# Step-size product of a gated state-space block: high and low weight columns side by side, with the next unit's two tiles computed block by block beside it

## The reference

```python
u = rms_norm(x, ln1[i]) * (1.0 + scale1) + shift1
...
proj = u @ w_in
gl, cb, cc, cx, z, xbc, dt = jnp.split(proj, split_at, axis=-1)
...
xbc = jax.nn.silu(causal_depthwise_conv(xbc, ssm_conv_w) + ssm_conv_b.astype(xbc.dtype))
...
dt = jax.nn.softplus(dt.astype(jnp.float32) + dt_bias.astype(jnp.float32))
a = -jnp.exp(a_log.astype(jnp.float32))
y = ssd_scan(xs * dt[..., None], dt * a, bs, cs)
```

## Time and profile before

| | us |
|---|---|
| median of 3 runs | 2229.18 (2227.27 to 2230.26) |
| the profiled execution, its own time | 2227.39 |
| its span in the trace | 2225.5 |
| PE busy | 2191.5 (98%) |
| VectorE busy | 1297.4 (58%) |
| ScalarE busy | 858.3 (39%) |
| mean granted clock of TensorE | 0.994 |

### The profile page before, as it was taken

One profiled execution on the slowest core, in us unless ns is written; L12 is line 12 of the kernel. 1 busy time (PEld: TensorE's weight loads), 2 busy tenths in 40 slices (PEclk: granted clock), 3 DMA queues, 4 the chain that ended last, 5 costly groups with the idle time before them and its releaser, 6 DMA issues.

```text
span 2225.5 us, 28686 instructions
## 1 busy us (share of the span) xinstructions
PE 2191.5 (98%) x10938; PEld 1829.6 (82%) x10938; DVE 1297.4 (58%) x1831; ACT 858.3 (39%) x1223; POOL 25.4 (1%) x24
## 2 busy tenths in 40 slices
PE   7999999999999999999999999999999999999998
PEld 5888888888888898888888888889878678888887
DVE  5677777777673475434475344354777756434344
ACT  5655555543222342322343222234455444222224
POOL 0000000000000000000000000000001000000000
PEclk9999999999999999999999999999999899999999
DMA  7423223224543334223223322223121012232321
GB/s 262 126 82 105 97 96 105 101 76 158 183 151 101 104 116 133 95 95 96 92 95 98 111 94 96 95 95 93 40 77 39 20 33 82 95 98 98 107 85 67
DMA packets 208141, 222.10 MB, mean 100 GB/s; under 512 B 9413, under 2 KB 200330, under 8 KB 205994
## 3 DMA queue, kind: packets, MB, share of 16 engines
q1 hardware_dynamic: 206362, 210.26, 29.1%
q10 hardware_dynamic: 1680, 10.49, 1.2%
HBM read 218.57 MB, written 2.16 MB: 99 GB/s over the span
## 4 chain that ended last, share of the span: by engine, by line
PE 93%; DVE 3%; DMA 2%; ACT 1%; issue 1%; ACTq 0%; DVEq 0%; SPq 0%
PE G L560 25%; PE G L561 25%; PE G L562 25%; PE G L611 2%; PE G L612 2%; PE G L613 2%; PE G L1050 1%; PE X L763 1%; PE X L1067 1%; DMA araw<-in_w_ada 1%; PE G L574 1%; PE G L576 1%; PE G L575 1%; PE X L1057 1%; PE X L1033 1%
## 5 line engine op out<-in xcount | busy, mean ns | idle before, releaser
L560 PE MATMUL G<-ahi,whi 128*128 128x512 f32 x1480 | 587.8, 397 | 0.1
L562 PE MATMUL G<-ahi,wlo 128*128 128x512 f32 x1480 | 577.8, 390 | 0.0
L561 PE MATMUL G<-alo,whi 128*128 128x512 f32 x1480 | 577.5, 390 | 0.0
L1874 DVE TENSOR_TENSOR wlo<-raw,whi 128x2048 fp32r<-128x2048 f32 (+3 forms) x172 | 386.9, 2249 | 237.4 <-ACT whi L1208 234.5
L1208 ACT ACTIVATE whi<-raw 128x2048 fp32r<-128x2048 f32 (+3 forms) x176 | 330.1, 1876 | 443.0 <-PE G L562 423.4
L560 PEld LDWEIGHTS G<-ahi,whi 128*128 128x128 f32 x1480 | 278.9, 188 | 58.8 <-issue 2.1
L561 PEld LDWEIGHTS G<-alo,whi 128*128 128x128 f32 x1480 | 279.0, 188 | 58.4 <-issue 1.9
L562 PEld LDWEIGHTS G<-ahi,wlo 128*128 128x128 f32 x1480 | 278.6, 188 | 58.6
L560 PE MATMUL G<-hhi,whi 128*128 128x512 f32 x784 | 305.8, 390 | 0.5 <-issue 0.5
L562 PE MATMUL G<-hhi,wlo 128*128 128x512 f32 x784 | 305.0, 389 | 0.0
L561 PE MATMUL G<-hlo,whi 128*128 128x512 f32 x784 | 305.0, 389 | 0.0
(11 more groups left out here) (422 smaller groups left out, 2844.8 us busy)
## 6 DMA issues: line engine op xcount, KB each, us to landing
raw<-in_w_in SPq DMA_DIRECT2D x43, 1024.0 KB, 5.1
raw<-in_w_up SPq DMA_DIRECT2D x38, 1024.0 KB, 5.3
raw<-in_w_down SPq DMA_DIRECT2D x32, 1024.0 KB, 5.1
raw<-in_w_gate SPq DMA_DIRECT2D x22, 1024.0 KB, 5.1
braw<-in_w_ada SPq DMA_DIRECT2D x12, 1024.0 KB, 5.3
raw<-in_w_in SPq DMA_DIRECT2D x20, 512.0 KB, 4.5
araw<-in_w_ada ACTq DMA_DIRECT2D x8, 1024.0 KB, 18.0
bc<-acum_dram SPq DMA_DIRECT2D x8, 1024.0 KB, 6.9
```

Source lines behind the costliest of these rows:

```text
L560: pe.matmul(bank[:], wh[:, j, f], rh[:, j, :], start=(j == 0), stop=False)
L561: pe.matmul(bank[:], wh[:, j, f], rl[:, j, :], start=False, stop=False)
L562: last = pe.matmul(bank[:], wl[:, j, f], rh[:, j, :], start=False, stop=(j == k - 1))
L1874: tt(wlo[s][:, 0:n], raw[s][:, 0:n], r32(whi[s][:, 0:n]), ALU.subtract).then_inc(lo_split, 1)
```

## The change

The step-size product takes two matmuls for each block instead of three. The high and the low part of its 32 weight columns now stand side by side in `whi[0]`, as 64 columns for each block: ScalarE writes the first 32, VectorE the last 32. One matmul with all 64 columns against `ahi` gives the high x high sum in rows 0 to 31 of G0 and the low x high sum in rows 32 to 63; a second one with the first 32 columns against `alo` adds to rows 0 to 31. The two halves are added when they are turned: `turn_dt` now takes, for each of the 4 token blocks, two ordinary fp32 matmuls of the copied tile (64 rows) with the two halves of the identity's columns, summed in PSUM, in place of one transpose. ScalarE's copy takes 64 rows instead of 32.

PE's order changes as well. The step-size product and both tiles of unit 1 are computed together, block by block: for each of the 8 blocks two step-size matmuls and three for each of the two tiles. The turn comes behind all of it. The local function `unit` of the ScalarE part is renamed `split_unit`, since it hid the helper `unit` that gives a view; that rename has no effect. The orders of ScalarE, VectorE, GpSimd and SyncE stay the same.

```diff
-            s = next_unit()
-            bank = take_g(2 * s)[0:HEADS, :]
-            wh, wl = unit(whi[s], KB, HEADS), unit(wlo[s], KB, HEADS)
-            for j in range(KB):
-                pe.wait_ge(act_ready, t["op"].now(j + 1))
-                pe.matmul(bank, wh[:, j, :], ahi[:, j, :], start=(j == 0), stop=False)
-                pe.matmul(bank, wh[:, j, :], alo[:, j, :], start=False, stop=False)
-                last = pe.matmul(bank, wl[:, j, :], ahi[:, j, :], start=False, stop=(j == KB - 1))
-            last.then_inc(tile_done, 1)
-            t["op"].add(KB)
+            def first_tiles():
+
+                s = next_unit()
+                bank, wd = take_g(2 * s), unit(whi[s], KB, 2 * HEADS)
+                sx = next_unit()
+                bank_x, wh, wl = take_g(2 * sx), unit(whi[sx]), unit(wlo[sx])
+                bank_y = take_g(2 * sx + 1)
+                for j in range(KB):
+                    pe.wait_ge(act_ready, t["op"].now(j + 1))
+                    if j:
+                        pe.matmul(bank[0:HEADS, :], wd[:, j, 0:HEADS], alo[:, j, :], start=False, stop=False)
+                    last = pe.matmul(bank[0:2 * HEADS, :], wd[:, j, :], ahi[:, j, :], start=(j == 0), stop=(j == KB - 1))
+                    if j == 0:
+                        pe.matmul(bank[0:HEADS, :], wd[:, j, 0:HEADS], alo[:, j, :], start=False, stop=False)
+                    if j == KB - 1:
+                        last.then_inc(tile_done, 1)
+                    for m, dst in enumerate((bank_x, bank_y)):
+                        f = slice(m * P, (m + 1) * P)
+                        pe.matmul(dst[:], wh[:, j, f], ahi[:, j, :], start=(j == 0), stop=False)
+                        pe.matmul(dst[:], wh[:, j, f], alo[:, j, :], start=False, stop=False)
+                        last = pe.matmul(dst[:], wl[:, j, f], ahi[:, j, :], start=False, stop=(j == KB - 1))
+                        if j == KB - 1:
+                            last.then_inc(tile_done, 1)
+                t["op"].add(KB)
+                return sx
...
                 for c in range(TB):
-                    last = pe.transpose(bank[:, c * HEADS:(c + 1) * HEADS], ss[0:HEADS, c * P:(c + 1) * P],
-                                        ident[0:HEADS, 0:HEADS])
+                    for half in range(2):
+                        last = pe.matmul(bank[:, c * HEADS:(c + 1) * HEADS], ss[0:2 * HEADS, c * P:(c + 1) * P],
+                                         ident[0:2 * HEADS, half * HEADS:(half + 1) * HEADS],
+                                         start=(half == 0), stop=(half == 1))
                 last.then_inc(aux_done, 1)
...
-                if gemm:
+                if dt:
+                    sx = first_tiles()
+                    turn_dt()
+                elif gemm:
                     sx = next_unit()
                     fm_tile(sx, 0, ahi, alo)
-                if dt:
-                    turn_dt()
...
-                if gemm:
+                if gemm and not dt:
                     fm_tile(sx, 1, ahi, alo)
...
-            act.activation(whi[0][:, 0:KB * HEADS], raw[0][:, 0:KB * HEADS], ACT.Copy).then_inc(hi_split, 1)
+            act.activation(unit(whi[0], KB, 2 * HEADS)[:, :, 0:HEADS], unit(raw[0], KB, HEADS), ACT.Copy)\
+                .then_inc(hi_split, 1)
...
-            act.activation(ss[0:HEADS, :], G[0][0:HEADS, :], ACT.Copy).then_inc(dt_ready, 1)
+            act.activation(ss[0:2 * HEADS, :], G[0][0:2 * HEADS, :], ACT.Copy).then_inc(dt_ready, 1)
...
-            n0 = KB * HEADS
-            tt(wlo[0][:, 0:n0], raw[0][:, 0:n0], r32(whi[0][:, 0:n0]), ALU.subtract).then_inc(lo_split, 1)
+            both = whi[0][:, 0:2 * KB * HEADS].rearrange("p (k n) -> p k n", k=KB)
+            tt(both[:, :, HEADS:2 * HEADS], raw[0][:, 0:KB * HEADS].rearrange("p (k n) -> p k n", k=KB),
+               r32(both[:, :, 0:HEADS]), ALU.subtract).then_inc(lo_split, 1)
```

More of the change, by code:

```diff
@@ L1321, in unit @@
                 return s
-            first = unit(2)
+            first = split_unit(2)
             act.wait_ge(prep_v, 1)
@@ L1380, in scan_turn @@
                 if gemm:
-                    s = (slot[0] if outp else unit(2)) if s is None else s
+                    s = (slot[0] if outp else split_unit(2)) if s is None else s
                     if t["xf"].i is not None or t["xf"].now():
@@ L1394, in scan_turn @@
                 if gemm:
-                    s = unit()
+                    s = split_unit()
                 def keys_in(m):
@@ L1465, in _ @@
             y_squares()
-            unit()
+            split_unit()
             t["tile"].add(2)
@@ L1544, in _ @@
             t["tile"].add(4)
-            second = unit()
+            second = split_unit()
             token_root(X[0], slice(2, TB), D)
             half_highs(1, 0, KB)
-            early = [second, unit()]
+            early = [second, split_unit()]
             def stream(hi, gain, k, twice=False):
@@ L1565, in ffn_turn @@
                 for u in range(4):
-                    s = early[u] if first and u < 2 else unit()
+                    s = early[u] if first and u < 2 else split_unit()
                     for m in range(2):
@@ L1626, in slab @@
                                 if k % 2 and u < 3:
-                                    unit(n=width if u < 2 else UNIT)
+                                    split_unit(n=width if u < 2 else UNIT)
                                     t["tile"].add(2)
@@ L1733, in _ @@
                 if u:
-                    unit(3 if u == 2 else 1)
+                    split_unit(3 if u == 2 else 1)
                 if u == 1:
```

39 lines of the change are left out of this document (19 added, 20 removed).

## The result

| | before | after |
|---|---|---|
| median us (runs) | 2229.26 (22) | 2232.31 (22) |
| lowest and highest | 2224.88 to 2232.15 | 2228.59 to 2234.47 |
| the profile's span | 2225.5 | 2232.5 |
| TensorE busy, us | 2191.5 | 2196.7 |

The kernel is 3.0 us slower. The ratio is 1.0013, with a 95% interval of 1.0008 to 1.0019: a small loss, measured clear of zero, and within the 0.2% that the prediction called no change. 2232.31 lies in the forecast range and 0.9 us above the forecast.

What follows compares the result with a forecast made beforehand. TensorE, busy 98% of the span, bounds the kernel. Fewer matmuls and no activation waits -4.1, turn and first wait +3.95, second wait +2.3: 2.2 us slower, 2229.18 to 2231.4 us; range 2226.8 to 2235.5.

Steps and rivals of the forecast that it cites:

- The chain: After the last step-size matmul (53.45): copy 53.88, unit 2's high part 54.65, low part to 58.96, B/C 59.0, Z unit 72.2.
- The two margins: In before, VectorE's low parts end ahead of TensorE's need: 6.2 us for unit 2 (B/C), 3.0 for unit 3 (Z).
- the signs of being wrong: B/C starting before 58 us, the Z unit before 71, or the granted clock showing 0.50 after 70 us.
- The layout of the step-size weights: New high and low splits, same 256 elements per partition: costed at nothing, with 0.90 us of VectorE idle time as cover.
- the first wait: TensorE behind the turn, waiting for unit 2's low part: some 2 us without work (1.6 to 2.8), B/C at 59.0.
- the second wait: TensorE after B/C, waiting for VectorE's low part of unit 3: 2.3 us, Z unit starting at 72.2.
- The mis-sized term: Start of the joint product on TensorE: first three matmuls 0.42 us apart, the rest 0.228, the 64th starting at 54.8.
- The turn: Eight fp32 matmuls for four transposes on TensorE: 1.5 us taken, bounds 0.9 to 2.1, ending at 56.9; no effect on the sum.
- a fall in the first wait: Clock rival: granted clock falls before B/C, costing at most what the second wait hides, 2.3 us of loss.
- The rival in which the clock falls behind the second wait: Clock falls before the Z unit: 3.4 us lost, 2234.8 us, chance 0.14; shorter stretch 1.7 us, 2233.1 us, chance 0.12.
- keep its lead: Rival: unit 2 does not wait for slot 0, B/C starts at 56.9; 2227.0 us, or 2226.3 with short turn; chance 0.05.
- The late low stretch: Rival: the 10 us at low clock from 1744.4 us falls otherwise, 5.0 us come back; 2226.4 us, chance 0.09.

Runs made afterwards that it cites:

- slot 0 free: The full change with the step-size weights in wlo of slot 0 instead of whi, so unit 2's high part precedes the step-size copy; 2231.84 us, ratio 1.0014 against before.
- the early low part: The full change with VectorE's low part of unit 3 moved ahead of the last three of six convolution steps; 2234.79 us, ratio 1.0019 against before.
- one tile: The full change with only one tile of unit 1 beside the step-size product and the turn midway in the second tile; 2227.98 us, ratio 0.9999 against before.
- the six kernels with the joint product side by side: The full change and five variants of it (order, useless matmuls or weight slot edited), both tiles still beside the step-size product; medians 2230.45 to 2234.79 us.
- the clock held: The full change with two useless full-size fp32 matmuls behind the turn, filling TensorE's first wait; 2232.38 us, ratio 1.0023 against before.
- joint alone: The change's order with both tiles beside the step-size product, but three step-size matmuls per block and four transposes as in before; 2234.34 us, ratio 1.0024 against before.

## Why the prediction was right

**The chain.** From the last step-size matmul to the Z unit the prediction had 53.45 to 72.2, 18.75 us. Measured: 55.40 to 74.13, 18.73. The two margins, which wait is last and where VectorE goes on without idle time came out as read. Of the signs of being wrong none came: B/C started after 58, the Z unit after 71, and from 66 to 90 us the granted clock is 1.00. The layout of the step-size weights, put at nothing, cost nothing: VectorE's low split takes 0.42 us as before. The experiment with slot 0 free shows that the first wait is slot 0, the one with the early low part that the second is VectorE's order, and the one with one tile that the kernel gets no slower when both margins are kept.

**The mis-sized term** is "the first three go at 0.42, as before; the rest at" 0.228. Eight went at the half clock. That is 1.0 us, and it stands in front of the chain and so moved everything. The step from the row was wrong: how many matmuls are slow is no property of the first three, it is the time until the clock rises, and that differs from profile to profile (3 to 13 matmuls in the six kernels with the joint product side by side, one profile of each). That it was three in before could as well have come again, as it did with slot 0 free. In before this can't be seen in the time, since the activations set the pace. In the change TensorE is full, so each microsecond at half clock costs half a microsecond. It explains 1.0 of the 1.3 us between the forecast 2.2 and the 3.5 at the mark. Another 0.2 is the pitch, 0.232 us for the 0.228 taken, and 0.1 the Z unit, 11.01 us for 10.88. The median lies nearer to the forecast, 3.0 us over before for 2.2. That difference of 0.9 us is smaller than the scatter of the runs, so how near it came is in part luck.

**The turn** took 1.97 us, within the bounds, 0.5 above the value taken. It had no part in the time, as predicted, because TensorE waited 1.9 us behind it. By the factor of four that the Trainium skill gives for the transpose mode with fp32 ("TensorE: Matmul & The Clock Gate", "Terms") the estimate had been 3.4. The trace disagrees: 0.25 us for one of these matmuls and 0.11 for a transpose of before, a factor of 2.3, and the measurement decides.

**The clock in the waits.** The prediction gave a fall in the first wait as hidden. It fell, at the end of that wait, and the second wait was 0.4 us instead of the forecast 2.3; with the clock held it was 2.0, and the Z unit started at the same distance from the step-size product. The rival in which the clock falls behind the second wait did not happen in the profile after, but it did with slot 0 free, at the price it was given for a short stretch (1.8 measured, 1.7 forecast).

**The other rivals.** TensorE did not keep its lead. The late low stretch did not go: it lasted longer in this profile (some 13 us from about 1747 for 10 from 1744.4), and its length differs between profiles in which nothing near it was changed.

## What to carry to other kernels

When work is put beside a product that is paced by its inputs, ask when that product will be finished and who waits for it: its end can start a chain of buffer releases whose margin is smaller than the idle time that was filled. Fill only as much as fits between two inputs; here five matmuls for each block kept the chain and gained 0 to 1.1 us at the mark, with no gain clear of zero in the time, and eight lost 3.5. And a stretch that waits for its inputs hides a low clock, so filling it is worth less than the count of matmuls says.

## What the runs showed of the hardware

- The granted clock fell to 0.50 at the end of a wait of only 1.9 us with the small matmuls of the turn ahead (after), about 1 us behind the end of one of 2.3 us with full-size matmuls ahead (slot 0 free early), and inside one of 3.4 us (joint alone). It did not fall in every kernel with such a wait: it stayed at 1.00 behind the 2.0 us wait of the kernel with the clock held, and behind those of 0.4 and 0.8 us.
- Eight plain fp32 matmuls of 64 x 128 weights with 32 moving columns take 1.97 us as 16 records, 0.12 us each. A transpose of 32 x 128 is one record of 0.11 us (0.43 us for 4).
- Copies out of PSUM take 0.59 us for 32 and for 64 partitions.
